# A hybrid decoder block on one core: tile 1's experts are chosen in the attention stage, and the first expert dot products are spread three to an item instead of four

## The reference, cut to what matters

```python
x = layer_norm(alpha * x + mix, ln1_g[l], ln1_b[l])
# peer_ffn(h = x):
q = einsum('bsd,dk->bsk', h, w_q)                 # 1024 -> 8 heads x 2 halves x 128
scores = einsum('bshcd,hcnd->bshcn', q, sub_keys)
s1, i1 = top_k(scores[..., 0, :], 16)
s2, i2 = top_k(scores[..., 1, :], 16)
top_s, pos = top_k(s1[..., :, None] + s2[..., None, :], 16)
ids = i1 * 128 + i2                               # at pos
gates = softmax(top_s)
act = gelu(h . u_tab[ids]) * gates
out = sum_k act * v_tab[ids]
```

## Time and profile before

| | |
|---|---|
| median of 3 runs | 3259.27 us (3256.12 to 3261.7) |
| the profiled execution | 3262.99 us, its span 3261.2 us |
| busy share of the span | PE 82%, DVE 68%, POOL 45%, ACT 17% |
| items of the attention, 512.5 to 845.1 us | DVE busy 249.56 of 332.60 us |
| its last steps, to 913.2 us | DVE busy 35.26 of 68.10 us |
| expert steps 0 to 17, to 1349.7 us | DMA engines busy 87%, 317 GB/s |
| granted TensorE clock over the span | 0.907 of full |

### The profile page before, as it was taken

The page is one execution under the profiler, slowest core; times in us unless marked ns, Lnnn a source line. Parts: engine busy times, 40 slices in busy tenths (PEclk is TensorE's granted clock), DMA queues, the critical chain, the costliest instruction groups (busy, mean ns, idle before and its releaser), DMA issues.

```text
span 3261.2 us, 30907 instructions
## 1 busy us (share of the span) xinstructions
PE 2669.5 (82%) x9137; PEld 1364.6 (42%) x9137; DVE 2201.8 (68%) x4895; ACT 559.1 (17%) x1267; POOL 1482.6 (45%) x1333
## 2 busy tenths in 40 slices
PE   8999994675668887657689999999999987878883
PEld 3454542443324555423334444444444443434441
DVE  3334577867648788678845766744444688888888
ACT  1231101332103777400000000100000000000000
POOL 0011004445334222344565555566656576675773
PEclk9999996887888899878889999999999989889996
DMA  4213226555479898898999999899999999999995
GB/s 146 87 52 139 91 84 231 178 199 194 187 285 344 310 331 320 296 358 313 331 394 373 385 376 404 326 407 398 396 404 397 377 407 407 406 407 371 404 409 191
DMA packets 310549, 987.81 MB, mean 303 GB/s; under 512 B 29936, under 2 KB 57840, under 8 KB 309616
## 3 DMA queue, kind: packets, MB, share of 16 engines
q0 software_dynamic: 184320, 671.17, 54.1%
q1 hardware_dynamic: 123440, 314.21, 25.6%
q10 hardware_dynamic: 2624, 0.46, 0.1%
HBM read 947.98 MB, written 37.75 MB: 302 GB/s over the span
## 4 chain that ended last, share of the span: by engine, by line
PE 24%; issue 15%; POOL 14%; DMA 10%; DVE 5%; ACT 2%; DVEq 1%; ACTq 1%; PEld 0%; POOLq 0%; PEldq 0%
POOL u_ring L1994 9%; PE part L2090 7%; PE hid L2071 6%; PE turn_ps L2063 4%; DMA v_ring<-in_peer_v_dram,ids_t 4%; PE acc L2128 4%; POOL v_ring L2021 4%; DMA v_ring<-in_peer_v_dram,ids_u 2%; DVE x_rows_in L2317 2%; POOL v_ring L2007 2%; PE part L2099 1%; ACT dense_sums L2168 1%; DMA u_ring<-in_peer_u_dram,ids_u 1%; DMA u_ring<-in_peer_v_dram,ids_t 1%; ACT dense_sums L2170 1%
## 5 line engine op out<-in xcount | busy, mean ns | idle before, releaser
L2090 PE MATMUL part<-room 128*128 128x512 f32 x1536 | 716.4, 618 | 198.1 <-DVE room L2398 186.2
L2422 DVE CUSTOM_DVE_ANT_0 u_ring<-u_ring,x_rows_in 128x1024 f32<-128x1024 f32 x512 | 618.7, 1223 | 314.9 <-DMA u_ring<-in_peer_u_dram,ids_u 305.2
L1994 POOL DMA_INDIRECT u_ring<-in_peer_u_dram,ids_u x512 | 580.0, 1133 | 469.3 <-DVE dots L2422 327.1
L2071 PE MATMUL hid<-x1t_dense,room 128*128 128x384 f32 x2048 | 692.6, 492 | 5.8 <-DMA room<-in_peer_ut_dram 4.6
L2007 POOL DMA_INDIRECT v_ring<-in_peer_v_dram,ids_t x344 | 368.1, 1070 | 384.3 <-PE acc L2128 269.9
L2090 PEld LDWEIGHTS part<-room 128*128 128x128 f32 x1536 | 302.2, 199 | 565.6 <-issue 346.0
L2071 PEld LDWEIGHTS hid<-x1t_dense,room 128*128 128x128 f32 x2048 | 387.4, 192 | 320.9 <-issue 80.8
L2317 DVE SCALAR_TENSOR_TENSOR x_rows_in<-v_ring,coef,x_rows_in 128x1024 f32<-128x1024 f32 x208 | 267.1, 1284 | 63.8 <-DMA v_ring<-in_peer_v_dram,ids_u 50.1
L2206 ACT ACTIVATE room<-hid 128x384 f32<-128x384 f32 x128 | 62.7, 490 | 1435.0 <-PE hid L2071 1435.0
L2021 POOL DMA_INDIRECT v_ring<-in_peer_v_dram,ids_u x208 | 234.7, 1129 | 76.5 <-issue 58.5
L1165 POOL DMA_INDIRECT u_rows<-in_peer_u_dram,ids_first x123 | 153.0, 1244 | 186.7 <-POOLq L1164 160.9
(11 more groups left out here) (368 smaller groups left out, 2809.0 us busy)
## 6 DMA issues: line engine op xcount, KB each, us to landing
room<-in_peer_ut_dram SPq DMA_DIRECT2D x128, 512.0 KB, 7.0
room<-in_peer_v_dram SPq DMA_DIRECT2D x128, 512.0 KB, 9.7
wq_pair<-in_peer_wq_dram SPq DMA_DIRECT2D x25, 2048.0 KB, 19.0
gate_grid<-room SPq DMA_DIRECT2D x6, 4096.0 KB, 13.8
room<-gate_grid SPq DMA_DIRECT2D x32, 768.0 KB, 17.3
w_ring<-in_w_in_dram SPq DMA_DIRECT2D x10, 2048.0 KB, 7.9
w_ring<-in_w_out_dram SPq DMA_DIRECT2D x4, 2048.0 KB, 8.2
u_ring<-in_peer_u_dram,ids_u POOLq DMA_INDIRECT x512, 10.6
```

What stands on the lines that cost most here:

```text
L1994: pool.indirect_dma_start(u_ring[:, n % U_RING, :], None, peer_u, bass.IndirectOffsetOnAxis(ap=ids_u[:, q, k:k + 1], axis=0))\
L2071: last = mm.matmul(hid[:, 0:DT], ud[:, c % UD_RING, k, :], x1td[:, k, :], start=(k == 0), stop=(k == KC - 1))
L2090: last = mm.matmul(part[k % 3][:], weights[:, n % 2, i, d * P:(d + 1) * P], vd[:, slot, half * 512:(half + 1) * 512], start=(i == 0), stop ...
L2422: vec.tensor_tensor_reduce(u_ring[:, n % U_RING, :], u_ring[:, n % U_RING, :], x1[:, q % 2, :], 1.0, 0.0, ALU.mult, ALU.add, dots[:, q % 2 ...
```

## The change

Three things are done.

1. The four pairs of heads of tile 1 are chosen in the attention. At n = 15, 19, 23, 27 (`choice`) PE multiplies tile 1's turned rows with a pair's query weights into `OP`, the bank of the output projection; one step later it turns them, another later it scores them. ACT copies each result, for n = 13 also tile 1's turned rows into the part of `q_t` that is no longer read. DVE runs `best_eight` and `next_eight` at lag 4 and `best_pairs` and `look_up` at lag 5, ahead of the step's products. SP loads the next pair's weights when a pair is scored. Scores, picks and best sums stay in `rows_kept`, a buffer that both blocks share.
2. Products go three to an item for the 28 items and four to a step after, so they end at n = 38, and the five more buffers serve from product 92 on.
3. The expert loop loses four steps: tile 2 is chosen from step 0, tile 3 from 4, tile 4 from 8, token groups stand at steps 2 to 13, `DENSE_AT` is 14, and every later entry is 4 less. Tile 0's quads are 2 at step 2 and 3 at each of the steps 3 to 12.

The names and the three-to-an-item rule:

```diff
+        CHOICE = 15
+        def choice(n, lag):
+            g, rest = divmod(n - CHOICE - lag, DA_HEADS)
+            return g if rest == 0 and 0 <= g < HEADS // 2 else None
...
-        SPARE_FROM = 4 * (items + 2)
+        SPARE_FROM = 3 * items + 4 * 2
...
+        def products_by(n):
+            return 3 * min(n, items) + 4 * max(n - items, 0)
...
-            return range(min(4 * n, FIRST_SLOTS), min(4 * n + 4, FIRST_SLOTS))
+            return range(min(products_by(n), FIRST_SLOTS), min(products_by(n + 1), FIRST_SLOTS))
```

SP, at the end of its loop over the tiles t of the attention:

```diff
+                    if 1 <= t <= HEADS // 2:
+                        g = t % (HEADS // 2)
+                        sp.wait_ge(wq_free, 1).then_inc(wq_free, -1)
...
```

with the loads of `wq_pair` and `keys_pair` behind it. PE, right behind `scores(n)`:

```diff
+                    if choice(n, 0) is not None:
...
+                        pe.wait_ge(wq_in, 16).then_inc(wq_in, -16)
+                        pe.wait_ge(op_free, 1).then_inc(op_free, -1)
+                        for c in range(KC):
+                            last = mm.matmul(OP[:], x1t_one[:, c // 2, c % 2, :], wq_pair[:, c, :], start=(c == 0), stop=(c == KC - 1))
+                        last.then_inc(q_done, 1)
+                    if choice(n, 1) is not None:
+                        pe.wait_ge(q_copied, 1).then_inc(q_copied, -1)
+                        for c in range(4):
+                            last = mm.transpose(OP[:, c * P:(c + 1) * P], q_one[:, c, :], ident[:])
+                        last.then_inc(qt_done, 1)
+                    if choice(n, 2) is not None:
+                        pe.wait_ge(qt_copied, 1).then_inc(qt_copied, -1)
+                        pe.wait_ge(keys_in, 16).then_inc(keys_in, -16)
+                        for c in range(4):
...
```

DVE, behind `tail(n, 8)` and ahead of the products:

```diff
+                    if choice(n, 4) is not None:
+                        dve.wait_ge(pair_for_dve, 1).then_inc(pair_for_dve, -1)
+                        best_eight(vec, dve, pairs, sc_one).then_inc(pair_free, 1)
+                        next_eight(vec, dve, pairs)
+                    if (g := choice(n, 5)) is not None:
...
+                        best_pairs(vec, dve, pairs, top_one[:, at].rearrange("p (h k) -> p h k", k=TOPK))
+                        look_up(vec, dve, pairs, picks_one[:, :, at].rearrange("p c (h k) -> p h c k", k=TOPK))
```

The tables of the experts:

```diff
-CHOSEN_AT = {1: 0, 2: 4, 3: 8, 4: 12, 5: 20, 6: 40, 7: 43}
...
+CHOSEN_AT = {2: 0, 3: 4, 4: 8, 5: 16, 6: 36, 7: 39}
...
-DENSE_AT = 18
...
+DENSE_AT = 14
...
-V_COUNTS = (2 * (3,) + 13 * (2,), (2,) + 30 * (1,), (2,) + 30 * (1,))
+V_COUNTS = ((2,) + 10 * (3,), (2,) + 30 * (1,), (2,) + 30 * (1,))
```

More of the change, by code:

```diff
@@ L1245, in _ @@
                         for half in range(2):
-                            if half and t >= 3:
+                            if half == 0 and choice(n, 3) is not None:
+                                pe.wait_ge(pair_for_pe, 1).then_inc(pair_for_pe, -1)
+                            elif half and t >= 3:
                                 pe.wait_ge(t_free[1], 1).then_inc(t_free[1], -1)
@@ L1303, in _ @@
                         act.sem_inc(mix_ready, 1)
+                    if choice(n, 0) is not None:
+                        act.wait_ge(q_done, 1).then_inc(q_done, -1)
+                        act_.activation(q_one, OP[:].rearrange("p (c n) -> p c n", c=4), ACT.Copy).then_inc(q_copied, 1)
+                    if choice(n, 1) is not None:
+                        act.wait_ge(qt_done, 1).then_inc(qt_done, -1)
+                        act_.activation(q_one, OP[:].rearrange("p (c n) -> p c n", c=4), ACT.Copy).then_inc(qt_copied, 1)
+                    if choice(n, 2) is not None:
+                        act.wait_ge(pair_scored, 1).then_inc(pair_scored, -1)
+                        act.sem_inc(wq_free, 1)
+                        act.wait_ge(pair_free, 1).then_inc(pair_free, -1)
+                        act_.activation(sc_one, OP[:], ACT.Copy)
+                        act.drain().then_inc(pair_for_pe, 1)
+                        act.sem_inc(pair_for_dve, 1)
             @block.vector
@@ L1707, in normed_at, with build_experts @@
     return NORM_AT.index(step - lag) if step - lag in NORM_AT else None
[L1710 removed]
+def build_experts(nc, x1_dram, x1t_dram, g_dram, ids_first, top_first, dots_first, wq, keys, y, peer_wq, keys_t, peer_u, peer_v, peer_ut,
                   ln2_g, ln2_b, out):
@@ L2149, in _ @@
                         d = DENSE.index(t)
-                        for i, src in enumerate((parts[:, d % 2, 0, :], gates[:, gates_row(t), :], parts[:, d % 2, 1, :])):
+                        picks = parts[:, d % 2, :, :] if d else picks_one
+                        for i, src in enumerate((picks[:, 0, :], gates[:, gates_row(t), :], picks[:, 1, :])):
                             last = mm.transpose(turn_ps[:, i * P:(i + 1) * P], src, ident[:])
```

88 lines of the change are left out of this document (60 added, 28 removed).

## The result

The changed kernel takes 3243.15 us in the median of 10 runs (3236.74 to 3251.39), the kernel before 3260.20 in 10 runs beside it (3254.78 to 3266.12). The ratio is 0.9949 with a 95% interval of 0.9936 to 0.9963: about half a per cent faster, 17 us. The profiled execution's span is 3240.0 us, 21.2 less than before, at a granted clock of 0.911 (before 0.907).

What follows compares the result with a forecast made beforehand. DVE bound part of the attention's steps; in the expert prefix no engine was full, with DMA at 87%. Items +19, last steps +30 and prefix -76 give -27 us: 3233 us, own range 3222 to 3243, whole range 3212 to 3256.

Steps and rivals of the forecast that it cites:

- Items, +19: Attention's 28 items: choices +36.3 us, fewer products -19, copies and lower clock +2, in all +19 us.
- choices with all that came with them: Attention items: three first and two second halves of choices on DVE, 36.3 us, plus 2 for ACT copies and clock.
- Query product: PE in the attention: 7.03 us, or 9.67 at lower clock, hidden under DVE in steps 19, 23, 27, barely in 15.
- Last steps, +30: Attention's last steps: products and choices fill DVE's waiting and products set the end, 98 us for 68, +30.
- Prefix, -76: Expert stage before the dense chunks: four steps fewer save 82 us, less 6 for lateness, so -76 us.
- I take 6 us for what still gets late: Expert prefix: allowance for late transfers, 6 us, with bounds 0 and 24 if each of ten steps loses 2.4.
- the 30 that the prediction named as a sign of being wrong: Expert steps 3 to 11: forecast 27 to 29 us each; over 30 us would make the prediction wrong.
- what is late then is the quad that PE waits for: Expert prefix: lateness falls on the quad's rows, and behind it on the query result's turning and DVE's choice.
- they fit by 5%: Ten expert steps with three quads: 105 MB need 381 GB/s, against 399 shown in steps 2 to 5.
- Rival (2): Expert prefix: the mix's DMA ceiling is lower, 355 GB/s, so 105 MB take 296 us; total 3247 us, chance 0.05.
- The rule that spoke against it: Expert prefix: the skill's HBM limit, about 358 GB/s per core, gives 293 us instead of 276, prefix gain 65.
- Beyond: Dense stage behind the prefix: same bytes, moved as a block, passes the 76 us to the end.

Runs made afterwards that it cites:

- experiment 7: Kernel before, with the query weights of turns 7 to 15 of the expert prefix loaded by half: 3259.08 us, ratio 0.9998 to the kernel before.
- experiment 5: Changed kernel, with the query weights of turns 4 to 11 of the expert prefix loaded by half: 3221.88 us, 0.9882 of the kernel before.
- experiment 6: Changed kernel, with each 4 MB store in the expert prefix issued one step later, behind the next query weights' load: 3237.11 us, 0.9930 of the kernel before.
- experiment 8: Changed kernel, with the query weights of turns 4 to 11 loaded by a quarter alone: 3223.14 us, 0.9877 of the kernel before.
- experiment 9: Changed kernel, with the first four stores of the gate grid writing half of their bytes: 3227.20 us, 0.9893 of the kernel before.
- experiment 1: Kernel before, with only the thinner product schedule, three an item; tile 1's choices stay in the expert stage: 3253.8 us, ratio 0.9985.
- Experiment 3: Changed kernel, with PE computing each of tile 1's query products in the attention twice: 3249.17 us, 0.9966 of the kernel before.
- experiment 10: Changed kernel, with five products moved between the output projection's halves and few left in DVE-bound steps: 3213.88 us, 0.9863 of the kernel before.

## Why the prediction was right

It gave 3233 us; the median is 3243, outside the forecast's own range by a hair and well inside the whole range. The direction and the mechanism were right; one term was off in size, one cost stood in no term, and one cause was named wrongly.

- **Items, +19.** The attention as a whole begins up to 5.5 us earlier or later from one execution to another (DVE's first row minimum at 507.0 to 512.5), so I count from that row to step 28. The items take 332.6 us before (336.0 in experiment 7, with the same attention) and 353.7 after (350.7 to 353.9 in experiments 5, 6, 8 and 9, with the same attention): +21.1 between the two profiles, +18 between the means. The terms by themselves: choices with all that came with them +37.7 to +41.0 (forecast 36.3, and 2 for copies and clock), products -16.3 to -19.9 (19).
- **A cost in no term.** Pool now makes a row of numbers for DVE's choice (`iota_one`) ahead of its first gather. First the kernel before, Pool and DVE, then the changed kernel:

```profile
510.94 1.18 POOL L1165 DMA_INDIRECT u_rows<-in_peer_u_dram,ids_first  x1 [81.67 <-POOLq L1164]
519.56 1.22 DVE L1350 CUSTOM_DVE_ANT_0 u_rows<-u_rows,x_first 128x1024 f32<-128x1024 f32 x1 [5.96 <-DMA u_rows<-in_peer_u_dram,ids_first]
```

```profile
508.05 0.14 POOL L1200 IOTA iota_one<- 128x16 int32 x1 [80.60 <-POOLq L339]
514.25 1.18 POOL L1196 DMA_INDIRECT u_rows<-in_peer_u_dram,ids_first  x1 [6.06 <-POOLq L1195]
523.48 1.23 DVE L1431 CUSTOM_DVE_ANT_0 u_rows<-u_rows,x_first 128x1024 f32<-128x1024 f32 x1 [11.67 <-DMA u_rows<-in_peer_u_dram,ids_first]
```

In all nine traces with the iota 5.9 to 6.8 us pass between it and the first gather, and DVE waits 11.1 to 11.7 us for its first row; in the three without it the wait is 6.0 to 6.5. Part of the 5 us comes back, as the next rows then lie ready: with three products a step, step 1 begins 16.0 to 17.3 us behind the first row minimum where it was 14.4 without the iota (experiment 1), so the cost there is 1.6 to 2.9 us. No run takes the iota alone away, so that it is the cause is read from the order of the rows and not shown. That the sum still came out near 19 is in part luck.

- **Query product.** It hides in steps 19, 23 and 27 and barely in step 15, as argued. Experiment 3 shows it.
- **Last steps, +30.** 99.4 us for the forecast 98. Products set the end, as said, with twelve of them behind the last norm.
- **Prefix, -76.** Measured -71.8 in this profile and -66 to -70 in those of the four others with the same prefix. This is the term that was mis-sized: the step "I take 6 us for what still gets late". Without any lateness the prefix was to take 432.2 - 82 = 350.2 us; it took 360.4 here and 362.0 to 366.0 in those four, so what got late was 10 to 16 us. The ten steps took 285.2 us and not 282 (they were to take 275.9 and the part of the 6 us that falls in them), steps 12 and 13 49.9 for 48.6. The ten steps take 28.5 us in the mean, as forecast, but four of them (4, 5, 8 and 9) take 30.2 to 31.4, over the 30 that the prediction named as a sign of being wrong: lateness came in pairs of steps and not evenly.
- **Its cause.** The forecast said "what is late then is the quad that PE waits for". It was the query weights, which have one buffer and so can't be asked for before the last product has read them, while the rows of a quad have a ring of three and are asked for a step ahead. In the trace the load of 1054.05 follows within 0.1 us on the end of the product before it (1046.94 + 7.03), so it had no slack. But experiment 6 shows that this mostly says where the lack of bytes shows: with the weights served first, the quads waited, and the prefix was as long.
- **The bytes** were right: 105 MB forecast for these ten steps, 373 GB/s for 285 us is 106. What was wrong is the conclusion "they fit by 5%". This stage, which needed 381 of 399 GB/s on average, didn't get through without waits; 285 us for 106 MB is where it settled, and 8 MB less gave 21 us (experiment 5) or some 12 to 15 (experiment 9). That its 4 MB stores and 2 MB loads come in bunches may be the reason; no run evens them out. Rival (2), a ceiling of 355 for the mix, was nearer in time but wrong in its figure: the mix moved 373.
- **The rule that spoke against it**, 358 GB/s for one core in the Trainium skill, "DMA: Bandwidth & Descriptors", Specifications, gave 293 us for these steps. They took 285 at a mean of 373 GB/s, so as a limit for a core that runs alone it is exceeded in this trace. By it the prefix would have given 65 us; by the rows, 76; it gave 72.
- **Beyond.** The dense stage passed all of it to the end, as assumed.

So where did the gain go? Leaving out four steps was to give 82 us and gave 72, as the bytes took some 10. The choices in the items took 38 to 41 and the thinner products gave 16 to 20 of them back. The last steps took 31: 54.5 us of DVE work (89.78 less 35.26) came into 32.8 us of idle time (68.10 less 35.26). Part of what was left unused was DVE's waiting for the output projection, which experiment 10 then filled.

## What to carry to other kernels

Work that is moved onto a waiting engine is free only if it is put into the waiting itself: here the same products cost 1.17 us each at the head of a DVE-bound step and nothing between two halves of a projection that DVE waits for. When steps are merged, add up their bytes before their instructions: these ten steps went with next to no waits for weights at 312 of the 399 GB/s that the trace had shown, and lost time when they needed 381. The waits showed first at the transfer with a single buffer. When such a wait is found, move the suspected transfer before believing in it, and read the whole stage: if the wait turns up elsewhere and the stage keeps its length, the sum counts for more than the order. And when time stamps of two executions are compared, count from a common row inside the stage, or the scatter of what ran before is read as an effect.

## What the runs showed of the hardware

- A DMA share of 0.97 didn't say by itself that bytes were the bound. With half of the weights the ten steps had 0.97 at 367 GB/s and PE waited for no transfer in them; with whole weights they had the same 0.97 at 373 GB/s and took 18 us more.
- A 2 MB load of weights in the prefix took 7.9 us to land at best and 24.2 behind a 4 MB store and the rows of another queue.
- In the changed kernel PE's waits of 4.96 and 4.39 us were followed by query products of 8.58 and 8.80 us in place of 7.03. When the waits were gone, the mean granted clock of the ten steps was 0.95 in place of 0.93 and the same matmuls were busy 5.4 us less, so that 12.8 us of waiting went with 18 us of time.
